# Modulation chains as the moving operand of their sums, and pooling moved from GpSimd to VectorE

## The chip, the cores and the metric

One core of one Trainium2 chip. The metric is the device time of one execution, in microseconds (us); the median of three runs stands for the kernel. The profile is of one further execution.

## The reference, cut to what matters

Two transformer stacks run one after the other on 256 tokens (X) of width 1024, the first with 256 context tokens (CTX) beside them. All is float32. The parts that the change touches are the modulation vectors of four sets (two layers of the first stack, two of the second), and the pooling branch of the first layer:

```python
mod = (silu_c @ ada_w[i] + ada_b[i])[:, None, :]      # ada_w[i]: 1024 x 6144
mod_c = silu_cc @ ada_w[i] + ada_b[i]
sh1, sc1, gt1, sh2, sc2, gt2 = jnp.split(mod, N_MOD, axis=-1)
...
for gi, w in enumerate(POOL_WINDOWS):                 # 2, 4, 8, 16
    lo = jnp.clip(t - w // 2, 0, L)
    hi = jnp.clip(t + w // 2, 0, L)
    ...
    mean = (jnp.take(csg, hi, axis=1) - jnp.take(csg, lo, axis=1)) / (hi - lo)[None, :, None]
    outs.append((mean - uf[..., sl]).astype(u.dtype) @ pool_w[gi])
```

A product of one vector (or of two, where the context needs its own) with a 1024 x 6144 matrix, four times over; and for each of four groups of 128 features a windowed mean less the value itself.

## The kernel before, in words

**Weights and queues.** All large weights come as blocks of 1 MB through a ring of four slots, in one written order (`block_order`, L215). SyncE issues the loads (`load_blocks`, L412): block j waits until block j - 4 is used. Each engine has a program of its own, written out at the end of the kernel; `step` marks an event on a semaphore and `wait_ge(*after(event))` waits for one. A `mod` block is 256 columns of a modulation matrix: 24 of them make a set. The order puts 16 further blocks of set 0 (after the first eight) between the blocks of the first projection (`ev_in`) and of the first output projection (`ev_out`), sets 1 and 2 into the first feed-forward network (`mlp1_0`, `mlp2_0`, in four quarters of an up and a down half, both segments, 512 tokens), and set 3 into the second (`mlp1_1` up, `mlp2_1` down, 256 tokens).

**Chains and sums.** Four of the first eight mod blocks are multiplied on TensorE (`mod_block`, L580). All others are a chain on VectorE (`mod_chain`, L594): the eight 128-row slices of the block, each times one column of silu(c), added up elementwise (L613, L616). With two vectors (set 0 and a third of set 1) the chain keeps one accumulator of 128 x 256 per vector. With one vector it keeps two accumulators, for even and odd slices, and adds them at the end (L620). TensorE then sums over the 128 partitions (`mod_sum`, L626): the accumulator is the stationary operand, 128 columns at a time, and one column of ones moves (L635). The result is one column of PSUM bank 7 per 128 outputs. Chains reuse their buffers: a chain waits for the sum of the chain two before it (the first eight) or four before it. `side_blocks` (L460) places the sums in TensorE's program ahead of the matmuls of the next block. `mod_vectors` (L660) adds the biases chunk by chunk on VectorE (L679), applies the gains (L687), and frees bank 7 for the next set.

**Split matmuls.** The large products run as three matmuls of rounded operands. ScalarE rounds a block (`high`, L506), VectorE makes the remainder (`low`, L515), and TensorE multiplies (`columns`, L537). VectorE's chains stand in block order ahead of the remainder of the block that follows them (`side_chains`).

**Pooling.** GpSimd (`pool_pool`, L1211) waits for the four pooled tiles of the first projection (`taken ev_in 3`), then runs for each of the four groups one to four doubling adds (L1225), a product with the inverse counts (L1230) and a subtraction (L1232). `pool_tensor` (after both attentions) multiplies the results.

**Attention.** `att_tensor`, `att_vector` and `att_scalar` run 16 units (head, half of the queries) each for the latent and then the context attention. In unit i VectorE takes the scores out of PSUM and finds the maxima (L1063 to L1076), then normalises unit i - 1 (L1083, L1097); ScalarE does the exponentials and copies; TensorE does the scores (L1013), transposes (L1023) and values (L1034). In the context attention TensorE also makes filling matmuls (L998).

**Norms.** A norm sums squares on TensorE (L786), takes the root on ScalarE (L802) and the reciprocal on VectorE (L809), and then adds the residual (L898, L903). `mod_vectors` for set 0, chunks 2 to 5, stands in VectorE's program between the first remainders of the network and that reciprocal.

## Time and profile before

| | |
|---|---|
| median of 3 runs | 2556.5 us (2555.28 to 2557.27) |
| the profiled execution | 2558.39 us |
| its span | 2556.6 us |
| TensorE busy (PE) | 2362.8 us, 92% of the span |
| VectorE busy (DVE) | 1715.2 us, 67% |
| ScalarE busy (ACT) | 1020.0 us, 40% |
| GpSimd busy (POOL) | 67.1 us, 3% |

The profile names engines PE, PEld (weight loads of TensorE), DVE, ACT, POOL and SP. A line such as L616 is the line of the kernel that issued the instruction; lines inside a helper serve all its callers. The chain of waits is followed back from the last instruction: each piece is what the end waited for at that time. A float32 matmul appears as two records, each with a weight load. Durations of matmuls in the timeline include their way through the array, so neighbours overlap; the chain of waits shows them from end to end. PEclk is the granted clock of TensorE as a share of 2.4 GHz.

### The profile page before, as it was taken

Reading aid. Unit: us, or ns where it says so; the run is one execution under the profiler, and the core shown is the slowest. Engines: PE = TensorE matmul, PEld = TensorE weight load, DVE = VectorE, ACT = ScalarE, POOL = GpSimd, SP = SyncE. Lnnn points to the kernel's source line nnn. Section 1 sums busy time; section 2 is a strip of 40 time slices with the busy share of each in tenths; the row PEclk is TensorE's granted clock in tenths of the full one; section 3 lists DMA queues with packets and bytes.
Section 4 is the critical chain, followed back from the end, with each engine's and each line's share of the span. In section 5 each row is a group of like instructions: output and inputs, shape, how many; then the busy total and the mean of one; then the engine's idle time right before and its main releaser. Section 6 shows DMA issues by size and latency. Waiting matters only on the chain.

```text
span 2556.6 us, 46809 instructions
## 1 busy us (share of the span) xinstructions
PE 2362.8 (92%) x20170; PEld 1952.1 (76%) x20170; DVE 1715.2 (67%) x3302; ACT 1020.0 (40%) x1893; POOL 67.1 (3%) x70
## 2 busy tenths in 40 slices
PE   6899989999998999999999889898989989998997
PEld 5675467888875578889887789894777888677886
DVE  5966779677646247887763777756356865745576
ACT  2225243323322224544432453334245653644465
POOL 0300000000000000000000000020000011000000
PEclk9899989999998999999999999899899999997999
DMA  7330426665542100000003577550056943003574
GB/s 310 133 131 1 158 106 222 230 256 216 213 155 75 57 1 3 3 4 3 11 4 118 200 273 294 188 182 1 9 206 230 345 165 132 1 1 132 181 303 191
DMA packets 47279, 348.02 MB, mean 136 GB/s; under 512 B 5248, under 2 KB 5248, under 8 KB 5728
## 3 DMA queue, kind: packets, MB, share of 16 engines
q1 hardware_dynamic: 45936, 334.52, 35.1%
q0 software_dynamic: 1136, 10.51, 1.0%
q8 instruction: 158, 2.59, 0.4%
q14 instruction: 49, 0.40, 0.0%
HBM read 343.96 MB, written 1.05 MB: 135 GB/s over the span
## 4 chain that ended last, share of the span: by engine, by line
PE 76%; DVE 16%; ACT 6%; issue 2%; DMA 1%; DVEq 0%; ACTq 0%; POOLq 0%
PE banks L537 23%; PE banks L932 9%; PE banks L1852 6%; DVE arena L616 3%; PE banks L2708 3%; PE banks L2709 3%; PE banks L2710 3%; PE banks L786 2%; PE banks L1718 2%; PE banks L1034 2%; PE banks L1013 2%; PE banks L1929 1%; PE banks L2739 1%; PE banks L2741 1%; PE banks L2740 1%
## 5 line engine op out<-in xcount | busy, mean ns | idle before, releaser
L616 DVE SCALAR_TENSOR_TENSOR arena<-weight_slots,silu_c,arena 128x256 f32<-128x256 f32 x776 | 328.1, 492 | 0.0
L515 DVE TENSOR_TENSOR moe_w_low<-weight_slots,moe_w_high 128x2048 fp32r<-128x2048 f32 x96 | 217.9, 2289 | 70.4 <-ACT moe_w_high L506 69.5
L932 PE MATMUL banks<-arena,weight_slots 128*128 128x256 f32 (+1 forms) x768 | 229.6, 457 | 13.5 <-DVE arena L1599 11.7
L932 PEld LDWEIGHTS banks<-arena,weight_slots 128*128 128x128 f32 x768 | 148.3, 194 | 88.7 <-issue 73.6
L506 ACT ACTIVATE mlp_w_high<-weight_slots 128x2048 fp32r<-128x2048 f32 x64 | 122.3, 1911 | 178.3 <-PE banks L537 105.4
L506 ACT ACTIVATE moe_w_high<-weight_slots 128x2048 fp32r<-128x2048 f32 x96 | 181.2, 1911 | 23.8 <-PE banks L2741 19.7
L515 DVE TENSOR_TENSOR mlp_w_low<-weight_slots,mlp_w_high 128x2048 fp32r<-128x2048 f32 x64 | 146.3, 2286 | 49.2 <-ACT mlp_w_high L506 49.1
L1852 PE MATMUL banks<-weight_slots,arena 64*64 64x64 f32 (+1 forms) x3648 | 147.0, 223 | 18.9 <-ACT arena L1872 13.3
L1852 PEld LDWEIGHTS banks<-weight_slots,arena 64*64 64x64 f32 x3648 | 138.9, 135 | 27.2 <-ACT arena L1872 15.2
L2708 PE MATMUL banks<-moe_w_high,slots_x 128*128 128x512 f32 x320 | 133.2, 416 | 11.8 <-DVE moe_w_low L515 11.8
L2709 PE MATMUL banks<-moe_w_low,slots_x 128*128 128x512 f32 x320 | 129.2, 404 | 0.0
L2710 PE MATMUL banks<-moe_w_high,slots_x 128*128 128x512 f32 x320 | 128.8, 403 | 0.0
L1117 ACT ACTIVATE arena<-arena 128x256 f32<-128x256 f32 (+2 forms) x160 | 71.9, 450 | 104.6 <-DVE arena L1076 104.6
L786 PE MATMUL banks<-arena,constants 128*128 128x256 f32 (+1 forms) x224 | 75.8, 476 | 20.3 <-ACT arena L830 20.3
L2080 ACT ACTIVATE weight_slots<-banks 128x512 f32<-128x512 f32 x80 | 46.9, 595 | 118.5 <-DVE weight_slots L2259 92.6
L1929 PE MATMUL banks<-weight_slots 64*64 64x64 f32 x2560 | 83.6, 220 | 9.2 <-DVE weight_slots L2296 9.2
L1034 PEld LDWEIGHTS banks<-arena 128*64 128x64 f32 (+2 forms) x520 | 55.6, 139 | 42.0 <-issue 23.6
L1929 PEld LDWEIGHTS banks<-weight_slots 64*64 64x64 f32 x2560 | 78.9, 135 | 11.2 <-DVE weight_slots L2296 11.2
L613 DVE TENSOR_SCALAR arena<-weight_slots,silu_c 128x256 f32<-128x256 f32 x184 | 58.0, 356 | 37.4 <-PE banks L635 18.3
L1034 PE MATMUL banks<-arena 128*64 128x128 f32 (+2 forms) x520 | 80.3, 285 | 2.6 <-ACT arena L1135 1.4
L2708 PEld LDWEIGHTS banks<-moe_w_high,slots_x 128*128 128x128 f32 x320 | 61.8, 193 | 25.8 <-ACT moe_w_high L506 9.7
L2296 DVE TENSOR_TENSOR weight_slots<-banks,constants 128x512 f32<-128x512 f32 x80 | 54.2, 688 | 40.4 <-PE banks L1852 40.4
(392 smaller groups left out, 5196.6 us busy)
## 6 DMA issues: line engine op xcount, KB each, us to landing
weight_slots<-weights SPq DMA_DIRECT2D x318, 1024.0 KB, 4.8
arena<-small POOLq DMA_DIRECT2D x1, 2560.0 KB, 9.0
arena<-x_t POOLq DMA_DIRECT2D x1, 2048.0 KB, 15.9
arena<-bias POOLq DMA_DIRECT2D x1, 2048.0 KB, 9.5
constants<-consts POOLq DMA_DIRECT2D x1, 1410.0 KB, 21.2
out_t<-arena SPq DMA_DIRECT2D x1, 1024.0 KB, 3.9
parameters<-params POOLq DMA_DIRECT2D x1, 775.0 KB, 9.2
arena<-pool_inv POOLq DMA_DIRECT2D x1, 512.0 KB, 10.4
```

The source lines that it names most:

```text
L506: nc.scalar.activation(self.pair(j)[0], slot(j, 0, SLOT), ACT.Copy).then_inc(*act.step("high", j))
L515: nc.vector.tensor_tensor(self.pair(j)[1], slot(j, 0, SLOT), self.pair(j)[0], ALU.subtract).then_inc(*v.step("used", j))
L537: ins = nc.tensor.matmul(out, self.pair(j)[part][:, at:at + P], x(k), start=start and n == 0 and k == 0, stop=stop and n == 2 and k == til ...
L616: nc.vector.scalar_tensor_tensor(a_, w, c, a_, ALU.mult, ALU.add).then_inc(*v.step())
L786: ins = nc.tensor.matmul(psum(SUMS_BANK[segs[-1]], 0, len(segs) * SEQ), cn("ones"), squares_of(key, segs, k), start=(k == 0), stop=(k == K ...
L932: ins = nc.tensor.matmul(psum(b, 0, w), slot(j, k, 256, i * P, P), moving(k), start=(k == 0), stop=(k == KT - 1))
L1034: ins = nc.tensor.matmul(psum(b, 0, P, rows), v, T[0:w, u % 2, i * P:(i + 1) * P], start=(i == 0), stop=(i == len(vs) - 1))
L1852: ins = nc.tensor.matmul(psum(b, n * width, width, r), lhs, rhs, start=(i == 0), stop=(i == len(ts) - 1))
L1929: ins = nc.tensor.matmul(psum(b, p * 64, 64, r), Z[r, p, :], XI[r, p, :], start=False, stop=True, skip_group_check=True)
L2708: nc.tensor.matmul(psum(b), x_hi, wh, start=(k == 0), stop=False)
L2709: nc.tensor.matmul(psum(b), x_hi, wl, start=False, stop=False)
L2710: ins = nc.tensor.matmul(psum(b), x_lo, wh, start=False, stop=(k == KT - 1))
```

## The change

- A chain's sum has the accumulators as moving operand (256 columns) and a 24-column matrix as stationary operand, which has ones in column n and zeros elsewhere. Chain n thus lands in row n of a 24-row block of PSUM bank 7, 256 columns per vector. With one vector TensorE adds both accumulators into the same row, and VectorE's add (L620) is gone. This holds for all chains but those of the first eight blocks.
- When the 24 rows of a set are there, VectorE copies them to SBUF (`mod_rows_vector`), in the place of the last chain's accumulators, and TensorE transposes them back into columns (`mod_turn`). `mod_vectors` then adds all biases of a vector in one instruction. The buffer of a set's last chain is free only after the turn.
- The block order in the first network puts all of set 1 ahead of the last block of the second down quarter, and the first block of set 2 behind the first up block after it.
- The pooling instructions run on VectorE, one after each of units 2 to 13 of the latent attention and 2 to 7 of the context attention. GpSimd keeps only the clearing of the padded tiles.
- A constant of 47 columns is added.

```diff
--- before.py
+++ after.py
@@ -44,7 +44,8 @@
 for _n, _w in (("ident", 128), ("ones", 128), ("block_ones", 128), ("swap", 128), ("cos", 256), ("sin", 256),
                ("causal", 128), ("cmp_mask", 2 * N_CMP), ("cmp_live", 2), 
                ("order", 2 * 128), ("first_level", 2 * 64), ("later_levels", 2 * 5 * 64), ("ident64", 64),
-               ("scan_keep", 512), ("tie", 4), ("eps", 2), ("heads", 30)):
+               ("scan_keep", 512), ("tie", 4), ("eps", 2), ("heads", 30),
+               ("one_row", 47)):
     _const(_n, _w)
 N_CONST = sum(w for _, w in CONST_COLS.values())
@@ -88,6 +89,7 @@
     c["tie"] = np.broadcast_to(np.array([4.0, 3.0, 2.0, 1.0]), (P, 4))
     c["eps"] = np.broadcast_to(np.array([RMS_EPS, GN_EPS]), (P, 2))
     c["heads"] = (np.arange(30)[None, :] == 14 + i[:, None] // HD)
+    c["one_row"] = np.broadcast_to(np.arange(47) == 23, (P, 47))
     out = np.concatenate([np.asarray(c[n], np.float64).reshape(P, w) for n, (_, w) in CONST_COLS.items()], 1)
     return np.ascontiguousarray(out.astype(np.float32))
@@ -216,8 +218,9 @@
     order = ["mod0"] * FIRST_MODS + ["ev_in"] * 2 + mixed(("ev_in", 6), ("mod0", 8)) + mixed(("ev_out", 4), ("mod0", 8))
     order += ["mlp1_0"] * 2 + mixed(("mlp1_0", 2), ("mod1", 3)) + mixed(("mlp2_0", 4), ("mod1", 7))
-    order += mixed(("mlp1_0", 4), ("mod1", 7)) + mixed(("mlp2_0", 4), ("mod1", 7))
-    order += (mixed(("mlp1_0", 4), ("mod2", 6)) + mixed(("mlp2_0", 4), ("mod2", 6))) * 2
+    order += mixed(("mlp1_0", 4), ("mod1", 8)) + mixed(("mlp2_0", 3), ("mod1", 6)) + ["mlp2_0"]
+    order += ["mlp1_0"] + mixed(("mlp1_0", 3), ("mod2", 6)) + mixed(("mlp2_0", 4), ("mod2", 6))
+    order += mixed(("mlp1_0", 4), ("mod2", 6)) + mixed(("mlp2_0", 4), ("mod2", 6))
     order += ["wr"] * 4 + ["wk"] * 4 + ["wv"] * 4 + ["wo"] * 4
     order += mixed(("mlp1_1", 16), ("mod3", 12)) + mixed(("mlp2_1", 16), ("mod3", 12))
     order += ["ev2_in"] * 12 + ["ev2_out"] * 4 + ["moe0"] * 48
@@ -568,12 +571,11 @@
             return (CTX, X) if m == 0 or (m == 1 and n < FIRST_MODS) else (X,)
-        def mod_bank(pe, m):
-            key = ("mod", m, 0)
+        def mod_bank(pe, m, part):
+            key = ("mod", m, part)
             if bank_state["holder"][7] != key:
                 if bank_state["holder"][7] is not None:
-                    held = bank_state["holder"][7]
-                    pe.wait_ge(*after("taken", "mod", held[1], 2 if held[1] == 0 else 0))
+                    pe.wait_ge(*after("taken", *bank_state["holder"][7]))
                 bank_state["holder"][7] = key
                 events.where[key] = 7
@@ -581,7 +583,7 @@
             m, n = mod_of(j)
             pe.wait_ge(*after("silu_c"))
-            mod_bank(pe, m)
+            mod_bank(pe, m, 0)
             pe.wait_ge(*after("block", j))
             for i in range(2):
                 t = 2 * n + i
@@ -599,7 +601,9 @@
             v.wait_ge(*after("block", j))
             slots = 2 if v.chains < 8 else 4
             if j >= FIRST_MODS and v.chains >= slots:
-                v.wait_ge(*after("mod_summed", *v.chained[v.chains - slots]))
+
+                m_, n_ = v.chained[v.chains - slots]
+                v.wait_ge(*(after("mod_turned", m_) if n_ == 23 else after("mod_summed", m_, n_)))
             vecs = mod_vecs(m, n)
             for k in range(KT):
                 w = slot(j, k, 256)
@@ -615,17 +619,55 @@
                         v.wait_ge(v.own[0], v.own[1] - 1)
                         nc.vector.scalar_tensor_tensor(a_, w, c, a_, ALU.mult, ALU.add).then_inc(*v.step())
             v.mark("used", j)
-            if len(vecs) == 1:
-                v.wait_ge(*v.own)
-                nc.vector.tensor_tensor(acc[:, 0], acc[:, 0], acc[:, 1], ALU.add).then_inc(*v.step())
             v.mark("mod_acc", m, n)
             if j >= FIRST_MODS:
                 v.chained.append((m, n))
                 v.chains += 1
+        def in_rows(m, n):
+
+            return m > 0 or n >= FIRST_MODS
+
+        def first_row(m):
+            return FIRST_MODS if m == 0 else 0
+
+        def mod_row(pe, m, n):
+
+
+            mod_bank(pe, m, part_of(m))
+            pe.wait_ge(*after("mod_acc", m, n))
+            acc = chain_sums[m, n]
+            pe.wait_ge(*after("consts"))
+            vecs = mod_vecs(m, n)
+
+            for a_, s in enumerate(vecs if len(vecs) == 2 else vecs * 2):
+                ins = nc.tensor.matmul(psum(7, s * 256, 256, ROWS_24), cn("one_row", 23 - n, 24), acc[:, a_],
+                                       start=(n == first_row(m) and a_ == 0), stop=True, skip_group_check=True)
+            ins.then_inc(*pe.step("mod_summed", m, n))
+
+        def mod_rows_vector(v, m):
+
+
+            v.stage("mod")
+            v.wait_ge(*after("mod_summed", m, 23))
+            at_ = 256 * mod_vecs(m, first_row(m))[0]
+            nc.vector.tensor_copy(rows_of(m)[:, at_:512], psum(7, at_, 512 - at_, ROWS_24)).then_inc(*v.step("mod_rows", m))
+
+        def mod_turn(pe, m):
+
+            pe.wait_ge(*after("mod_rows", m))
+            for s in mod_vecs(m, first_row(m)):
+                for i in range(2):
+                    ins = nc.tensor.transpose(psum(7, (2 * s + i) * 24, 24), rows_of(m)[:, s * 256 + i * P:s * 256 + i * P + P],
+                                              cn("ident", 0, 24, ROWS_24))
+            ins.then_inc(*pe.step("mod_turned", m))
+
         def mod_sum(pe, m, n):
-            mod_bank(pe, m)
+            if in_rows(m, n):
+                mod_row(pe, m, n)
+                return
+            mod_bank(pe, m, 0)
             pe.wait_ge(*after("mod_acc", m, n))
             acc = chain_sums[m, n]
             pe.wait_ge(*after("consts"))
@@ -644,6 +686,12 @@
         chain_sums.update({mod_of(j): OUT_ACC[:, i % 4] for i, j in enumerate(rest[8:16])})
         chain_sums.update({mod_of(j): MACC[:, i % 4] for i, j in enumerate(rest[16:])})
+        ROWS_24 = slice(0, 24)
+        part_of = lambda m: 2 if m == 0 else 0
+
+        def rows_of(m):
+            return chain_sums[m, 23][ROWS_24].rearrange("p a b -> p (a b)")
+
         def side_chains(v, j_next):
             while v.at_block < j_next:
@@ -660,7 +708,8 @@
         def mod_vectors(v, m, chunks=range(6)):
             v.stage("mod")
-            v.wait_ge(*after("mod_summed", m, 4 * chunks[-1] + 3))
+            rows = in_rows(m, 4 * chunks[0])
+            v.wait_ge(*(after("mod_turned", m) if rows else after("mod_summed", m, 4 * chunks[-1] + 3)))
             v.wait_ge(*after("params"))
             M = MOD[m]
             src = psum(7, 0, 2 * MOD_TILES).rearrange("p (t s) -> p t s", s=2)
@@ -672,7 +721,14 @@
             else:
                 gains[1] = (pr("norm1_g2", (m - 2) * KT, KT), 1.0)
                 gains[4] = (pr("norm2_g2", (m - 2) * KT, KT), 1.0)
-            for chunk in chunks:
+            for s in (mod_vecs(m, 4 * chunks[0]) if rows else ()):
+
+                n0, n1 = 4 * chunks[0], max(n for n in range(24) if s in mod_vecs(m, n)) + 1
+                part = M[:, 2 * n0:2 * n1, s].rearrange("p (n i) -> p i n", i=2)
+                b = bias_at[:, 2 * n0:2 * n1].rearrange("p (n i) -> p i n", i=2)
+                got = psum(7, 48 * s, 48).rearrange("p (i n) -> p i n", i=2)[:, :, n0:n1]
+                nc.vector.tensor_tensor(part, got, b, ALU.add).then_inc(*v.step())
+            for chunk in (() if rows else chunks):
                 vecs = mod_vecs(m, 4 * chunk)
                 t, s = slice(chunk * KT, (chunk + 1) * KT), slice(vecs[0], vecs[-1] + 1)
                 b = bias_at[:, t].unsqueeze(2).to_broadcast([P, KT, len(vecs)])
...
@@ -1208,28 +1264,34 @@
             g.wait_ge(*after("read", KT - 1))
             g.eng.dma_start(SORT, small[:, 6656:6656 + N_SORT]).then_inc(*g.step("sorting", by=16, sem="sorting_loaded"))
-        def pool_pool(g):
+        def pool_pads(g):
             g.stage("pooling")
             nc.gpsimd.memset(UP, 0.0).then_inc(*g.step("pads"))
-            g.wait_ge(*after("taken", "ev_in", 3))
-            g.wait_ge(*after("pool_inv"))
-            for gi in range(4):
-                u = UP[:, gi]
-                src, shifts = u, []
-                for lv in range(gi + 1):
-                    dst = PT3[:, lv % 2]
-                    up, down = (0, 1) if lv == 0 else (1 << (lv - 1), 1 << (lv - 1))
-                    lo, hi = 1 << lv, 288 - (1 << lv)
-                    g.wait_ge(*g.own)
-                    nc.gpsimd.tensor_tensor(dst[:, :, lo:hi], src[:, :, lo + up:hi + up],
-                                            src[:, :, lo - down:hi - down], ALU.add).then_inc(*g.step())
-                    src = dst
-                g.wait_ge(*g.own)
+
+        def pool_steps():
+
+
+            return [(gi, lv) for gi in range(4) for lv in range(gi + 3)]
+
+        def pool_vector(v, gi, lv):
+
+            u = UP[:, gi]
+            src = u if lv == 0 else PT3[:, (lv - 1) % 2]
+            if (gi, lv) == (0, 0):
+                v.wait_ge(*after("taken", "ev_in", 3))
+                v.wait_ge(*after("pool_inv"))
+            v.wait_ge(*v.own)
+            if lv <= gi:
+                up, down = (0, 1) if lv == 0 else (1 << (lv - 1), 1 << (lv - 1))
+                lo, hi = 1 << lv, 288 - (1 << lv)
+                nc.vector.tensor_tensor(PT3[:, lv % 2][:, :, lo:hi], src[:, :, lo + up:hi + up],
+                                        src[:, :, lo - down:hi - down], ALU.add).then_inc(*v.step())
+            elif lv == gi + 1:
                 inv = PINV[:, gi].unsqueeze(1).to_broadcast([P, 2, SEQ])
-                nc.gpsimd.tensor_tensor(PD[:, gi], src[:, :, 16:272], inv, ALU.mult).then_inc(*g.step())
-                g.wait_ge(*g.own)
-                nc.gpsimd.tensor_tensor(PD[:, gi], PD[:, gi], u[:, :, 16:272], ALU.subtract).then_inc(*g.step("pooled", gi))
+                nc.vector.tensor_tensor(PD[:, gi], src[:, :, 16:272], inv, ALU.mult).then_inc(*v.step())
+            else:
+                nc.vector.tensor_tensor(PD[:, gi], PD[:, gi], u[:, :, 16:272], ALU.subtract).then_inc(*v.step("pooled", gi))
         def pool_tensor(pe):
             pe.stage("pooling")
@@ -1419,6 +1481,8 @@
                         ins.then_inc(*pe.step("x02_part", q, g))
                         if i == 1:
                             pe.mark("multiplied", j)
+                        if q % 2 and g == KT - 2:
+                            mod_turn(pe, 1 + q // 2)
                         if q == 3 and g >= 3:
                             sums_tensor(pe, "y_x02", BOTH, g - 3)
                 if q == 1:
@@ -1465,6 +1529,9 @@
             v.stage("mlp0")
             for n in range(32):
                 q, r = divmod(n, 8)
+                if n % 16 == 15:
+                    mod_rows_vector(v, 1 + n // 16)
+                    v.stage("mlp0" if n == 15 else "mlp0b")
                 MLP0.low(v, n + MLP0.ahead)
                 if r < 4:
                     for f in (8 * q + 2 * r, 8 * q + 2 * r + 1):
@@ -1509,9 +1576,10 @@
                 pe.mark("x12_down", g)
                 if g >= 2:
                     sums_tensor(pe, "y_x12", ONE, g - 2)
+            side_blocks(pe, block_of["ev2_in"][0], 0)
+            mod_turn(pe, 3)
             for g in range(KT - 2, KT):
                 sums_tensor(pe, "y_x12", ONE, g)
-            side_blocks(pe, block_of["ev2_in"][0], 0)
         def mlp_split_scalar(act):
@@ -1558,6 +1626,8 @@
             for i in range(16):
                 MLP.low(v, 16 + i + MLP.ahead)
             side_chains(v, block_of["ev2_in"][0])
+            mod_rows_vector(v, 3)
+            v.stage("mlp_down")
             EV2.low(v, 0)
...
@@ -3257,7 +3327,7 @@
         def _(eng):
             g = queue(eng, "gpsimd")
             loads_pool(g)
-            pool_pool(g)
+            pool_pads(g)
             load_low_rank(g)
             ev2_pool(g)
             od_pool(g)
@@ -3284,6 +3354,7 @@
             project_tensor(pe, "x01", "ev_out", lambda k: CAT[:, :, k, :], cat_ready, BOTH,
                            banks=range(6),
                            then=y_sums(pe, "x01", BOTH, lambda: side_blocks(pe, block_of["mlp1_0"][0], 0)))
+            mod_turn(pe, 0)
             x_sums_tensor(pe, "n2_0", [X, CTX])
             mlp0_tensor(pe)
             x_sums_tensor(pe, "n1_1", ONE)
@@ -3400,11 +3471,16 @@
             EV_IN.low(v, 0)
             low_vector(v, "n1_0", 0, 0, BOTH, BOTH[::-1])
             ev_in_vector(v)
-            att_vector(v, LAT)
-            att_vector(v, CON)
+            pooling = pool_steps()
+            def pool_next(n):
+                for _ in range(n):
+                    pool_vector(v, *pooling.pop(0))
+            att_vector(v, LAT, {i: lambda: pool_next(1) for i in range(2, 14)})
+            att_vector(v, CON, {i: lambda: pool_next(1) for i in range(2, 8)})
             v.stage("norm")
             MLP0.low(v, 0)
             MLP0.low(v, 1)
+            mod_rows_vector(v, 0)
             mod_vectors(v, 0, range(2, 6))
             v.stage("norm")
             for seg in (X, CTX):
```

## Rows read from the trace of the kernel before

**Rows 1.** Busy time by stretch, all engines; from, length, then busy us (instructions).

```profile
core 0: us, PE busy (x) PEld busy (x) DVE busy (x) ACT busy (x) POOL busy (x), PEclk, DMA share, GB/s
100.00:125.00 25.00, 16.65 (x82) 13.90 (x80) 25.00 (x30) 5.51 (x5) 16.29 (x13) 0.89 0.14 45
...
460.00:560.00 100.00, 99.58 (x465) 82.64 (x464) 74.99 (x150) 29.18 (x34) 0.00 (x0) 1.00 0.63 236
```

**Rows 2.** Timeline, first projection: start, us, engine, line, what, count, [idle before].

```profile
84.89 5.63 DVE L616 SCALAR_TENSOR_TENSOR arena<-weight_slots,silu_c,arena 128x256 f32<-128x256 f32 x14
...
95.87 2.60 DVE L613 TENSOR_SCALAR arena<-weight_slots,silu_c 128x256 f32<-128x256 f32 x2
...
98.39 19.13 DVE L616 SCALAR_TENSOR_TENSOR arena<-weight_slots,silu_c,arena 128x256 f32<-128x256 f32 x14
...
117.57 1.05 PE L635 MATMUL banks<-constants,arena 128*128 128x1 f32 x8 [3.34 <-DVE arena L616]
...
123.63 1.87 PE L635 MATMUL banks<-constants,arena 128*128 128x1 f32 x8 [5.01 <-DVE arena L616]
```

**Rows 3.** Chain of waits, first projection: start, us, what, records.

```profile
125.84 13.01 PE banks L537 x48
138.85 0.79 PE banks L635 x8
139.63 11.05 PE banks L537 x48
...
163.10 1.68 PE banks L635 x16
```

**Rows 4.** Chain of waits, first norm after attention.

```profile
332.18 2.61 PE banks L635 x24
334.79 3.49 PE banks L786 x4
...
338.81 1.76 DVE arena L809
...
340.67 1.29 DVE arena L898 x2
...
342.75 0.60 DVE arena L898
```

**Rows 5.** Timeline, VectorE in two latent units and one context unit.

```profile
202.24 0.42 DVE L1063 TENSOR_SCALAR arena<-banks 128x256 f32<-128x256 f32 x1 [0.40 <-PE banks L1013]
...
204.90 0.42 DVE L1063 TENSOR_SCALAR arena<-banks 128x256 f32<-128x256 f32 x1 [0.40 <-PE banks L1013]
...
238.33 0.42 DVE L1063 TENSOR_SCALAR arena<-banks 128x256 f32<-128x256 f32 x1 [0.91 <-PE banks L1013]
```

**Rows 6.** Busy time by stretch, first norm after attention; columns as in rows 1.

```profile
334.70:335.50 0.80, 0.80 (x2) 0.43 (x3) 0.64 (x7) 0.00 (x0) 0.00 (x0) 0.50 1.05 440
```

**Rows 7.** Groups by line: count, busy us, mean ns, idle before.

```profile
L635 PE MATMUL banks<-constants,arena 128*128 128x1 f32 x480 | 60.4, 245 | 9.6 <-DVE arena L616 8.3 <-DVE modulations L679 1.2
...
L620 DVE TENSOR_TENSOR arena<-arena 128x256 f32<-128x256 f32 x64 | 27.2, 425 | 2.2
```

**Rows 8.** Chain of waits, both networks and the output projection between them.

```profile
562.57 0.47 DVE modulations L679 x6
...
563.08 0.61 PE banks L635 x4
...
574.72 0.79 PE banks L635 x8
...
586.55 0.34 PE banks L635 x4
...
1388.11 3.45 PE banks L932 x16
...
1459.09 0.42 DVE arena L620
...
1581.71 5.86 PE banks L537 x48
```

**Rows 9.** Busy time by stretch of L635 alone, second network's down half.

```profile
1550.00:1640.00 90.00, 5.53 (x44) 6.08 (x44) 1.00 0.80 298
```

More of the change, by code:

```diff
@@ L989, in fill_ready @@
             if held is not None and held[0] == "mod":
-                pe.wait_ge(*after("taken", "mod", held[1], 2 if held[1] == 0 else 0))
+                pe.wait_ge(*after("taken", *held))
             elif held is not None:
@@ L2651, in moe_tensor @@
             held = bank_state["holder"][7]
-            pe.wait_ge(*after("taken", *((*held[:2], 2 if held[1] == 0 else 0) if held[0] == "mod" else held)))
+            pe.wait_ge(*after("taken", *held))
             def unread(n):
```

## The prediction

> **What bounds the kernel now.** I first read the busy time by stretch, to see which engine fills which stage. In most of the first feed-forward network TensorE is busy for 99.6 of 100 us at full clock, with VectorE at 75: what is added to TensorE there lands on the end of the kernel, what is taken from VectorE does not [rows 1]. The stretch from 100 to 125 us is the opposite: TensorE is busy for 16.65 of 25 us, VectorE for all 25, and GpSimd, nearly idle elsewhere, for 16.29 [rows 1]. The timeline shows why. Fourteen multiply-adds of a modulation chain take 5.63 us as a rule, but 19.13 us from 98.39 on, and the two products ahead of them 2.60 us where they otherwise need some 0.6: exactly while GpSimd pools [rows 2]. TensorE then sits idle for 3.34 us and again for 5.01 us before it has the sums [rows 2], and when it resumes, 48 matmuls take 13.01 us where the next block's take 11.05, because the granted clock had fallen to the lower level [rows 3].
>
> **Pooling off GpSimd, in the projection.** Without the pooling, a chain of two vectors costs 6.1 us (5.6 + 0.5). VectorE's order is chain 3 (begun at 95.87 today), chain 4, rounding remainder of block 4. Chain 3 ends near 102. Chain 4 has two buffers and waits for the sum of chain 2, which TensorE makes after block 2, near 103 (114.2 less one block of 11.05); so it ends near 109.2 and the remainder near 111.5. TensorE ends block 3 at 114.2 (117.57 less the 3.34 idle) [rows 2], so it no longer waits: it sums two chains (1.7 us) and starts block 4 at 116.0 instead of 125.84. That is 9.9 us, and 2.0 us more for the warm clock: **-11.8 us** [rows 3]. I went on through the block order for chains 5 to 8: each ends before TensorE needs it, so the gain should stay. Bounds: -8 (chains a little late again) and -12.5.
>
> **Pooling onto VectorE, in attention.** Ten adds, four products and four subtractions move. VectorE needs 0.60 us of pitch for a two-input instruction of 512 elements, and 0.69 until its result stands: two take 1.29 [rows 4]. Up to 572 elements make that 0.66, and each waits for its own engine's last result, those 0.09 more: 0.75 us. Twelve of them come one per unit in the latent attention, six in the context attention. A latent unit takes 2.66 us (from 202.24 to 204.90), of which VectorE idles 0.40 until the scores are there [rows 5]; that idle figure counts to the end of the last instruction, so a unit becomes 2.26 + 0.09 + 0.60 to 0.66, about 2.94: 0.28 more. The first two units are slower anyway, and about 0.2 us of lead is used up first: 10 x 0.28 - 0.2 = **+2.6 us**. In the context attention the idle time is 0.91 us a unit [rows 5], more than 0.75: nothing. It costs 0 if the pitch hides better, and 18 x 0.75 = +13.5 if nothing does.
> The Trainium skill (VectorE: DVE Perf Modes, section on the TRN2 errata) gives a float32 tensor_tensor of N elements (N + 151)/0.96 ns, an estimated 0.75 us for 572. The rows give a close figure as duration, 0.69 for 512; I use the shorter pitch where nothing waits.
>
> **The sums of chains.** Before the change a chain half is the stationary operand, loaded 128 columns at a time against one column of ones. The profile has two records per float32 matmul. 480 records are 240 matmuls: four for each two-vector chain, two for a one-vector chain (64 of these, by the 64 halves added on VectorE), [rows 7]. On the chain of waits a pair of one-vector chains costs 0.79 us and a single one 0.34 [rows 8]; a two-vector chain costs 0.79 and a pair 1.68 [rows 3]. After the change each chain of either kind is two matmuls with 256 moving columns, four records. The nearest row is the plain float32 matmul with 256 moving columns: 16 records in 3.45 us, 0.216 each [rows 8]. So each chain costs 0.86 us, a pair 1.73. The 24-column load should hide.
> - Two-vector chains (24): 0.79 to 0.86, or 1.68 to 1.73; about **+0.6 us**.
> - One-vector chains in the first network (40). On the chain of waits stand 15 pairs and 7 singles, 14.2 us; three more hide where TensorE waits for ScalarE at the start of a down half. By the new order I count 16 pairs and 4 singles on the path: 16 x 1.73 + 4 x 0.86 = 31.1. **+16.9 us.** TensorE has no slack there [rows 1], so this is the largest term. Ends: +3.4 (rival A) and +19.
> - The new order lets an up block follow the second down quarter before any chain of the next set. TensorE now waits there for VectorE's add and six modulation adds until 563.08, 1.2 us [rows 8]: **-1.2 us**.
> - Second network, down half: 11 sums (44 records) [rows 9], each 0.34 to 0.86, on a TensorE that is busy throughout: **+5.7 us**.
> - Second network, up half: the other 13. There VectorE is in the path: chain, add of the halves, remainder, then TensorE. The removed add is 0.42 us plus its wait [rows 8], and the chain of waits crosses about ten; TensorE's longer sums fall into its waits for that remainder. **-3.5 us**, between -4.4 and +2 should TensorE take over.
> - Turning the rows back: 8 records for each of the first two modulation sets, 4 for the other two, at 0.1 each (as the small ones above). Sets 1 to 3 lie on the path: 0.8 + 0.35 + 0.35 = **+1.5 us**. VectorE's copies of the rows come beside a tile's worth of matmuls, so I cost them at nothing; if that cover went, about 0.6 us each.
>
> **The first norm after attention.** TensorE makes 24 tiny records in 2.61 us, then 4 wide ones in 3.49 us, twice the usual time [rows 4]: the granted clock is 0.50, the 1.2 GHz level, right after the tiny ones [rows 6]. With 256 columns moving the sums cost the same 2.6 us, and I expect the full clock, 1.7 us less. Against it, set 0 must now be turned (0.85 us) after the last sum, and VectorE has to make the modulation vectors (some 0.6 us) before its reciprocal at 338.81 [rows 4], where they were made earlier, under the sums. Together 338.2: **-0.6 us**. If the clock still falls: +2.0. If turning hides: -1.8.
> The Trainium skill (TensorE: Matmul & The Clock Gate, Part 4) says that PE-mode transposes do not count as busy for the clock; that would leave the norm where the second end has it, and no row here tells it.
>
> Nothing changes on the weight queue but the order of blocks; GpSimd's later loads come after the first network anyway.
>
> **Sum:** -11.8 + 2.6 + 0.6 + 16.9 - 1.2 + 5.7 - 3.5 + 1.5 - 0.6 = +10.2 us. The profiled execution took 2558.4, so 2568.6; the median of the runs is 2556.5, 1.9 lower, so **2566.7 us**.
>
> **Rivals.**
> A. *The wide sums are cheap (faster).* If a record with a narrow stationary operand runs like the one-pass matmuls with 256 columns, 48 in 5.86 us or 0.122 each [rows 8], a chain costs 0.49 us. The first network then adds 16 x 0.98 + 4 x 0.49 - 14.2 = 3.4, the down half 1.7, and the two-vector chains give back some 7: 13.5 + 4.1 + 7.6 less than above, about -15 us, **2541.5**. It decides from about 0.18 us a record downward, where the sum reaches zero. For it: nothing shows 24 stationary columns. Against: every float32 row with 256 or 512 columns goes by the moving columns alone. Chance 0.12.
> The Trainium skill (TensorE: Matmul & The Clock Gate, Back-to-back issue gap) gives 262 cycles, 109 ns, for 256 columns without telling float32 apart; by it a pair costs an estimated 0.87 us and the sum comes out faster still, near 2537. The float32 row shows twice that.
> B. *VectorE becomes the bound of attention.* If its units get all 0.75 us, with ScalarE and TensorE strung behind it: +13.5 in place of +2.6, **2577.6**. For: 0.40 us idle only. Against: the context units idle 0.91. Chance 0.11.
> C. *Covers and clock pay more.* If the attention hides its steps (-2.6), the norm gives 1.2 more, and the extra sums of a quarter of the places fall into waits (-4): +2.4, **2559**, within 0.2%. Chance 0.15.
> D. *The pooling was not what slowed VectorE.* Then the -11.8 is missing: +22, **2578.5**. Against: slow and fast chains change over with GpSimd's work. Chance 0.04.
>
> **Numbers.** The forecast has 0.58. Its own terms spread over about 2562 to 2573. A measurement of this kernel can tell some 0.2%, 5.1 us, from no change: slower is above 2561.6, faster below 2551.4. Slower: 0.58 + 0.11 + 0.04 = 0.73; same 0.15; faster 0.12. The range from 2557 to 2577.5 takes in case C and the near side of B, and leaves out A and D and a little more.
>
> **What would show it.** Right: no stretch of slow multiply-adds near 100 us, block 4 starting near 116; latent units of about 2.9 us; sums as x4 or x8 groups of 0.86 or 1.73 us on the chain, the first network some 16 us longer; the second network's up half shorter and its down half longer. Wrong: sums of 0.5 us a chain, units still at 2.66 or beyond 3.4, a new wait of TensorE for the row copies, or an up half bound by TensorE.

## The result, and the profile after

| | before | after |
|---|---|---|
| median of the runs | 2556.28 us (2555.28 to 2557.27, 4 runs) | 2581.41 us (2577.56 to 2583.37, 4 runs) |
| the profiled execution | 2558.39 us | 2583.36 us |
| its span | 2556.6 us | 2581.3 us |

The ratio is 1.0096, 95% interval 1.0084 to 1.0108: the change costs 25 us, where +10 had been forecast. First the page of the changed kernel, busy time by engine.

```profile
PE 2407.2 (93%) x20086; PEld 1931.8 (75%) x20086; DVE 1686.9 (65%) x3244; ACT 1022.7 (40%) x1893; POOL 42.1 (2%) x52
```

VectorE has 28 us less to do and GpSimd 25 us less; TensorE has 44 us more, and TensorE is what counts. Its chain of waits in the first projection (start, us, what, records), to be held against [rows 2, 3]:

```profile
89.30 0.97 PE banks L644 x4
90.27 11.15 PE banks L540 x48
...
113.53 1.84 PE banks L644 x8
115.37 11.10 PE banks L540 x48
```

L540 are the split matmuls, L644 the new sums. The gaps and the slow stretch of 13.01 us are gone, and block 4 starts at 115.37 (125.84 before, 116.0 forecast). The timeline of VectorE in the same place has every chain at its usual pace:

```profile
94.50 5.63 DVE L620 SCALAR_TENSOR_TENSOR arena<-weight_slots,silu_c,arena 128x256 f32<-128x256 f32 x14
102.50 0.61 DVE L617 TENSOR_SCALAR arena<-weight_slots,silu_c 128x256 f32<-128x256 f32 x2 [2.36 <-PE banks L644]
```

It is now VectorE that waits for TensorE (2.36 us), not the other way round. The same chain of waits in the first norm after attention [rows 4], in the first network and in the up half of the second [rows 8]:

```profile
326.55 2.70 PE banks L644 x12
329.25 1.91 PE banks L842 x4
332.25 1.67 DVE arena L865
...
436.30 1.84 PE banks L644 x8
438.14 11.10 PE banks L540 x48
...
558.21 0.35 PE banks L661 x4
558.57 16.54 PE banks L540 x72
575.10 1.84 PE banks L644 x8
...
1453.39 0.97 PE banks L644 x4
1454.36 5.94 PE banks L540 x48
...
1468.59 0.76 DVE hidden_low L1624 x2
1469.36 0.53 DVE arena L617 x2
1469.88 2.38 DVE arena L620 x6
1472.26 2.22 DVE mlp_w_low L518
...
1474.52 6.02 PE banks L540 x48
```

L661 are the transposes that turn the rows, L842 the norm's own sums, L865 its reciprocal. A pair of sums takes 1.84 us where 1.73 was forecast, a single one 0.97 where 0.86 was. The reciprocals serve as marks in both kernels, so the time can be told stage by stage. "First attention" is the latent and the context attention of the first layer together, up to the first matmul of the pooling. The first network runs from the last of the three reciprocals of its norm (353.7 us before, 347.05 after) to the reciprocal of the next norm (758.5 and 772.7). The second network (from 1418.9 and 1433.2) and the stages of the second stack are also counted between reciprocals. The two columns on the right are the changed kernel's two profiled executions (the second is the run `changed_again` below):

| stage | before | after | again |
|---|---|---|---|
| start to first attention's first scores | 176.39 | 164.82 | |
| first attention | 86.5 | 91.7 | 88.6 |
| reciprocal of the first norm stands at | 338.8 | 332.2 | |
| first network | 404.8 | 425.6 | 424.7 |
| second network | 220.9 | 226.5 | 226.4 |
| second stack's first attention | 182.4 | 185.0 | 184.9 |
| first expert network | 235.5 | 237.0 | 237.0 |

### The profile page after: what moved, and what is told of

Read it like the earlier page. It is cut to its first block, busy times and chain, and to the rows that moved or that the text cites. A ratio compares the mean times of both kernels' runs of the same rounds, so it can differ in the third digit from the quotient of the medians.

```text
span 2581.3 us, 46560 instructions
## 1 busy us (share of the span) xinstructions
PE 2407.2 (93%) x20086; PEld 1931.8 (75%) x20086; DVE 1686.9 (65%) x3244; ACT 1022.7 (40%) x1893; POOL 42.1 (2%) x52
## 4 chain that ended last, share of the span: by engine, by line
PE 79%; DVE 13%; ACT 6%; issue 1%; DMA 1%; DVEq 0%; ACTq 0%; POOLq 0%
PE banks L540 26%; PE banks L988 9%; PE banks L1922 6%; PE banks L644 3%; PE banks L2778 3%; PE banks L2779 3%; PE banks L2780 3%; PE banks L842 2%; PE banks L1788 2%; PE banks L1090 2%; PE banks L1069 2%; PE banks L1999 1%; PE banks L2809 1%; PE banks L2811 1%; PE banks L2810 1%; DVE arena L620 1%
## 5 line engine op out<-in xcount | busy, mean ns | idle before, releaser
L620 DVE SCALAR_TENSOR_TENSOR arena<-weight_slots,silu_c,arena 128x256 f32<-128x256 f32 x776 | 315.3, 483 | 0.0
L988 PE MATMUL banks<-arena,weight_slots 128*128 128x256 f32 (+1 forms) x768 | 229.4, 457 | 13.5 <-DVE arena L1669 11.8
L1922 PE MATMUL banks<-weight_slots,arena 64*64 64x64 f32 (+1 forms) x3648 | 147.0, 223 | 19.1 <-ACT arena L1942 13.5
L842 PE MATMUL banks<-arena,constants 128*128 128x256 f32 (+1 forms) x224 | 75.0, 472 | 20.3 <-ACT arena L886 20.3
L617 DVE TENSOR_SCALAR arena<-weight_slots,silu_c 128x256 f32<-128x256 f32 x184 | 56.5, 351 | 49.5 <-PE banks L644 30.5
L1999 PEld LDWEIGHTS banks<-weight_slots 64*64 64x64 f32 x2560 | 78.9, 135 | 11.2 <-DVE weight_slots L2366 11.2
L644 PE MATMUL banks<-arena,constants 128*24 128x256 f32 x352 | 87.2, 382 | 0.0
## 6 DMA issues: line engine op xcount, KB each, us to landing
arena<-x_t POOLq DMA_DIRECT2D x1, 2048.0 KB, 16.6
```

The lines of the kernel that those rows point to most:

```text
L620: nc.vector.scalar_tensor_tensor(a_, w, c, a_, ALU.mult, ALU.add).then_inc(*v.step())
L644: ins = nc.tensor.matmul(psum(7, s * 256, 256, ROWS_24), cn("one_row", 23 - n, 24), acc[:, a_], start=(n == first_row(m) and a_ == 0), sto ...
L988: ins = nc.tensor.matmul(psum(b, 0, w), slot(j, k, 256, i * P, P), moving(k), start=(k == 0), stop=(k == KT - 1))
L1922: ins = nc.tensor.matmul(psum(b, n * width, width, r), lhs, rhs, start=(i == 0), stop=(i == len(ts) - 1))
L1999: ins = nc.tensor.matmul(psum(b, p * 64, 64, r), Z[r, p, :], XI[r, p, :], start=False, stop=True, skip_group_check=True)
```

## The experiments

All times are medians in us; each ratio is to the kernel before, run on the same chip beside it.

**The pooling alone.** `pool_only` is the kernel before with the pooling part of the diff and nothing else. `sums_only` is the changed kernel with the pooling back on GpSimd. `pool_gap` takes the 18 instructions to another place, all at once ahead of the first unit:

```diff
-            att_vector(v, LAT, {i: lambda: pool_next(1) for i in range(2, 14)})
-            att_vector(v, CON, {i: lambda: pool_next(1) for i in range(2, 8)})
+            for step_ in pool_steps():
+                pool_vector(v, *step_)
+            att_vector(v, LAT)
+            att_vector(v, CON)
```

> The kernel before with the pooling part alone of the change (sums and block order as before). Theory 1 (the two parts add up, each at the price read in the changed kernel's trace): the attention's end shifts by -6.4 us there (-11.6 in the projection, +5.2 in the latent attention), so 2550, ratio 0.9975. Rival (the latent attention's extra 2.6 us over the 2.6 forecast is a matter of when the clock rises and differs from run to run): 2545 to 2551, and the latent units are 2.95 us either way. Rival (moving the pooling is itself what made the changed kernel slow, by clock dips later on): over 2560.

> The changed kernel with the pooling back on GpSimd: sums, turns and block order of the change alone. Theory 1: +20.7 us in the first network, +6.1 in the second, and up to +4 of later differences: 2583 to 2588, ratio 1.0105 to 1.0125. Rival (the later +4 us come from the sums through the clock and belong to this part): 2588. Rival (sums and pooling hurt only together): below 2575.

> The kernel before with all 18 pooling steps on VectorE in one go between the last remainder of the first projection and the first attention unit, where VectorE sat idle for 17.6 us before L1063. Theory 1: 18 x 0.75 = 13.5 us fit in the gap, the latent units are back at 2.66 us, so only the projection's gain is left: 2556.3 - 11.6 = 2544.7, ratio 0.9955. Rival (the shift of the start by itself costs what the clock gives, the pooling steps having nothing to do with it): latent attention some 2.6 us longer than before all the same, 2547.

Measured: `pool_only` 2546.82, ratio 0.9965 (0.9952 to 0.9977), 9.3 us faster than before; `pool_gap` 2544.74, 0.9955 (0.9938 to 0.9971); `sums_only` 2590.50, 1.0136 (1.0119 to 1.0153), 9.1 us slower than the changed kernel and 2.5 above what was expected of it. The timeline of VectorE in `sums_only` has the slow chain back:

```profile
94.48 2.60 DVE L617 TENSOR_SCALAR arena<-weight_slots,silu_c 128x256 f32<-128x256 f32 x2
97.00 19.15 DVE L620 SCALAR_TENSOR_TENSOR arena<-weight_slots,silu_c,arena 128x256 f32<-128x256 f32 x14
```

So the pooling part is worth some 9 us with either kind of sums, and the sums cost 34. With all 18 steps ahead of the attention, that takes 86.6 us, as before; with one in each unit it takes 91.6 (`pool_only`), of which some 3 us come from the clock, told below. The whole is 2.1 us faster in `pool_gap`, though the two intervals overlap. The timeline of VectorE shows where the steps go, first in `pool_only`, then in `pool_gap`:

```profile
165.15 0.42 DVE L1063 TENSOR_SCALAR arena<-banks 128x256 f32<-128x256 f32 x1 [17.61 <-PE banks L1013]
```

```profile
160.32 0.69 DVE L1238 TENSOR_TENSOR arena<-arena 128x512 f32<-128x512 f32 x1
164.91 0.42 DVE L1063 TENSOR_SCALAR arena<-banks 128x256 f32<-128x256 f32 x1 [3.90 <-PE banks L1013]
```

VectorE idles 17.61 us until the first scores are there. All the pooling fits into that with 3.90 us to spare.

**How much is the second matmul of a chain?** `one_half` lets VectorE add the halves again and TensorE sum one:

```diff
+            if len(vecs) == 1:
+                v.wait_ge(*v.own)
+                nc.vector.tensor_tensor(acc[:, 0], acc[:, 0], acc[:, 1], ALU.add).then_inc(*v.step())
...
-            for a_, s in enumerate(vecs if len(vecs) == 2 else vecs * 2):
+            for a_, s in enumerate(vecs):
```

> The changed kernel, but VectorE adds the two halves of a one-vector chain as before and TensorE sums one of them: 2 records in place of 4. Theory 1 (a sum costs 0.216 us a record plus about 0.11 once per group): a single costs 0.54 in place of 0.97, a pair 0.97 in place of 1.84; 36 chains on the path of the first network give back 15.6 us, the second network 5 to 9: 2557 to 2561. Rival (the cost is per chain, in the change of operands, and not per record): a single stays above 0.75, and the whole above 2568.

Measured: 2561.30, 1.0020 (1.0011 to 1.0030). The first network takes 409.0 us, 16.6 less than in the changed kernel. Its chain of waits there has a pair in four records in place of eight:

```profile
457.79 0.97 PE banks L647 x4
458.77 11.14 PE banks L540 x48
```

16.6 us is 38 times 0.43 us (two records of 0.216), and that network has 40 one-vector chains: the price per record with 256 columns moving, which the main term was built on, holds.

**Is the 24-column load free?** The four kernels below change only the number of stationary columns, and the place of the 47-column constant in its table. The added columns are other constants, and the rows of PSUM that they fill are never read. `wide_stationary`:

```diff
-                ins = nc.tensor.matmul(psum(7, s * 256, 256, ROWS_24), cn("one_row", 23 - n, 24), acc[:, a_],
+                ins = nc.tensor.matmul(psum(7, s * 256, 256), cn("one_row", 23 - n, 128), acc[:, a_],
```

`narrow_last` has 128 columns for sets 0 to 2 and 24 for set 3, `wide_last` the reverse, `stationary_64` has 64 for all.

> The changed kernel with 128 stationary columns in a sum in place of 24 (the columns beyond the 24 hold other constants, their rows of PSUM are never read). Theory 1 (a group of sums costs 0.97 and 1.84 us and not 0.86 and 1.73 because of the narrow load: it cannot be taken under the matmul before, and the next wide load not under it): groups fall to 0.86 and 1.73, the matmuls behind them to 11.05 and 5.86, some 60 groups on the path: 7 to 10 us faster than the changed kernel, 2572 to 2575. Rival (the extra is the change of operand type between rounded and plain float32, which only showed less with one moving column): groups stay at 0.97 and 1.84, 2581.

> 128 stationary columns in the sums of sets 0 to 2, 24 in those of set 3 (second network). Theory 3 (24 stationary columns cost about 0.11 us in the group and 0.2 in the matmuls behind it, wherever they are; the last 4 us come from the narrow sums too): the first network as in the wide run (418.0 us from mark to mark), the second network 226.5 in place of 220.7. The second stack's stages are 2.6 and 1.5 us longer if the last narrow sums before them decide: 2569 to 2570; if earlier ones do, as in the wide run: 2565.5.

> The mirror image: 24 columns in sets 0 to 2, 128 in set 3. Theory 3: the first network 425.6 us, the second 220.7; the second stack's stages as before if the last narrow sums decide (2569), 4 us longer if earlier ones do (2573).

> 64 stationary columns in all sums. Theory 3a (any stationary operand narrower than the full 128 columns keeps loads from being taken under the neighbouring matmuls): as with 24 columns, groups of 0.97 and 1.84, 2579 to 2581. Theory 3b (the price goes by the number of columns): halfway, near 2570. Rival (only the smallest loads are affected): 2560.

| | stationary columns, sets 0 to 2 / set 3 | median | ratio | first network | second network |
|---|---|---|---|---|---|
| changed kernel | 24 / 24 | 2581.41 | 1.0096 (1.0084 to 1.0108) | 425.6 | 226.5 |
| stationary_64 | 64 / 64 | 2575.06 | 1.0080 (1.0063 to 1.0097) | 425.4 | 227.0 |
| narrow_last | 128 / 24 | 2569.42 | 1.0052 (1.0035 to 1.0069) | 416.9 | 225.7 |
| wide_last | 24 / 128 | 2567.82 | 1.0051 (1.0034 to 1.0067) | 424.6 | 220.6 |
| wide_stationary | 128 / 128 | 2559.71 | 1.0011 (1.0002 to 1.0021) | 418.0 | 220.7 |

More than five times as many columns make the kernel 21.7 us faster, where 7 to 10 had been expected. Between the two profiles 13.4 us lie in the two networks (7.6 and 5.8), 1.8 and 1.2 in the projections ahead of and behind the first attention; 2.9 in that attention and 4.0 in two stages of the second stack, whose code does not differ, go with the clock, told below. Each network goes by the width in its own stage and not by the other's; the same code differs by 1.1 us between two kernels (418.0 and 416.9). With 64 columns the networks are no faster than with 24. That `stationary_64` is 6.3 us below the changed kernel as a whole is seen in the same stages that go with the clock: its profile has 88.5 us for the first attention, and the two later stages as before the change. The chain of waits of `wide_stationary` in the first network:

```profile
442.18 1.73 PE banks L643 x8
443.90 10.90 PE banks L539 x48
```

and that of `stationary_64`:

```profile
445.46 1.87 PE banks L643 x8
447.33 11.10 PE banks L539 x48
```

With 128 columns a pair costs exactly the forecast 1.73 us, and the 48 matmuls behind it 10.90; with 24 it is 1.84 and 11.10, with 64 1.87 and 11.10. That is 0.31 us for each group, and the 25 groups on the first network's path make 7.8 of the measured 7.6 us (425.6 less 418.0). The timeline of the changed kernel's weight loads (PEld), and then of its matmuls, at one pair:

```profile
462.11 1.42 PEld L644 LDWEIGHTS banks<-arena,constants 128*24 128x24 f32 x8 [0.35 <-issue]
463.95 1.68 PEld L540 LDWEIGHTS banks<-both_high,mlp_w_high 128*128 128x128 f32 x8 [0.42 <-DVE arena L617]
...
462.11 1.91 PE L644 MATMUL banks<-arena,constants 128*24 128x256 f32 x8
463.95 2.11 PE L540 MATMUL banks<-both_high,mlp_w_high 128*128 128x512 f32 x8
```

and the same views of `wide_stationary`:

```profile
454.41 1.72 PEld L643 LDWEIGHTS banks<-arena,constants 128*128 128x128 f32 x8
456.15 1.79 PEld L539 LDWEIGHTS banks<-both_high,mlp_w_high 128*128 128x128 f32 x8
...
454.64 1.89 PE L643 MATMUL banks<-arena,constants 128*128 128x256 f32 x8
456.18 2.19 PE L539 MATMUL banks<-both_high,mlp_w_high 128*128 128x512 f32 x8
```

With 128 columns the loads run on without a break: the first load of the sums stands 0.23 us ahead of its matmul. With 24 the loads stand idle for 0.35 and 0.42 us at the two changes of width, and load and matmul are recorded as starting together. The idle time stands where the stationary width changes (the second is put down to VectorE's L617, though no such wait stands there with 128 columns). That a load of another width is not taken under the running matmul is my reading of these rows; the cost by width is measured.

**What else could it be?** `const_only` is the kernel before with the unused 47-column constant, which moves the addresses behind it. `changed_again` is the changed kernel once more, for a second profile.

> The kernel before with the 47 unused constant columns alone, which move every buffer behind them by 188 bytes. Theory 2 (the last 4 us of the change, 2.6 in the second stack's first attention and 1.5 in the first expert network, where the granted clock falls after identical instructions, come with the moved addresses): the same two stages are longer by 2.6 and 1.5 us, 2560. Rival (they come with the sums or with how the clock's window happens to lie, not with the constant): stages as before, 2556.

> The changed kernel once more, for a second profile. Theory 2 and the sums' theory alike: the second stack's first attention is again 2.6 us and the first expert network 1.5 us longer than before. Rival (chance in the clock): at least one of them is as before. The latent attention begins at half clock again for some 22 us, or, if that is chance, for 11 us, which would make it 2.6 us shorter.

Measured: `const_only` 2556.88, 0.9998 (0.9988 to 1.0007), with stages as before: addresses are out. `changed_again` 2579.26, 1.0086 (1.0066 to 1.0106). Its first attention took 88.6 us where the first profile had 91.7. One stretch of 10 us of it in the changed kernel's first profile (columns as in [rows 1]):

```profile
175.00:185.00 10.00, 10.00 (x30) 5.67 (x30) 6.30 (x16) 3.56 (x11) 0.00 (x0) 0.51 0.01 2
```

and of its second:

```profile
175.00:185.00 10.00, 9.92 (x50) 5.92 (x49) 8.52 (x23) 4.48 (x12) 0.00 (x0) 0.93 0.01 2
```

The same program stays at the lower clock (0.51) for most of this stretch in one execution and leaves it early (0.93) in the other: 3 us, by execution.

**The new order, and a version that beats both.** `gap_order` is `pool_gap` with the new block order and the old sums. `gap_order_up` goes on from it: for the 13 chains of the second network's up half, where VectorE is in the path, VectorE's add goes, and TensorE adds the second half in the old form, with one moving column:

```diff
-            if len(vecs) == 1:
+            if len(vecs) == 1 and not (m == 3 and n < 13):
...
+            both = m == 3 and n < 13
             for i in range(2):
                 for a_, s in enumerate(mod_vecs(m, n)):
                     at_ = 2 * (2 * n + i) + s
                     ins = nc.tensor.matmul(psum(7, at_, 1), acc[:, a_, i * P:(i + 1) * P],
-                                           cn("ones", 0, 1), start=True, stop=True)
+                                           cn("ones", 0, 1), start=True, stop=not both)
+                    if both:
+                        ins = nc.tensor.matmul(psum(7, at_, 1), acc[:, 1, i * P:(i + 1) * P],
+                                               cn("ones", 0, 1), start=False, stop=True)
```

> Pooling in one go before attention (as in the run pool_gap), sums as before, and the block order of the change. Theory 1: TensorE no longer waits 1.2 us for the modulation vectors of set 1 after the second down quarter, and the sums cost 0.79 and 0.34 as before: 2544.7 - 1.2 = 2543.5. Rival (the six modulation adds return as a wait at the next sum): 2544.7.

> The run gap_order, with VectorE's add of the halves taken away in the 13 chains of set 3 that lie in the second network's up half; TensorE adds both halves there, but with one moving column as before (8 records in place of 4, 0.79 us in place of 0.34). Tests the term of -3.5 us by itself: if VectorE's add is on the path there, the second network falls from 220.9 us by 3 to 4.4 us and the kernel to 2539.5; rival (TensorE takes over as the bound, as it did in the changed kernel): 220 us or more, 2543.

Measured: `gap_order` 2543.05, 0.9945 (0.9929 to 0.9962); its first network takes 402.7 us against 404.9 in `pool_gap`, so the order is worth 2.2 us there, though between the whole kernels 1.7 us is within the spread. `gap_order_up` 2539.11, 0.9930 (0.9913 to 0.9946), the lowest median of all, 17 us below the kernel before; its interval overlaps that of `gap_order`, but its second network takes 215.7 us against 220.9. Its chain of waits there:

```profile
1451.78 6.02 PE banks L538 x48
1457.81 0.12 PE banks L637 x2
1457.92 0.22 PE banks L640 x2
...
1458.59 5.86 PE banks L538 x48
...
1478.39 6.01 PE banks L538 x48
```

A chain's sum, from 1457.81 to 1458.59, is 0.78 us with one column moving, 0.19 less than the 0.97 of the changed kernel, and the matmuls behind it take 5.86 instead of 5.94.

## Why the prediction was right or wrong

| step | forecast | measured |
|---|---|---|
| pooling off GpSimd, to the first scores | -11.8 | -11.6 and -11.2 |
| pooling in the attention | +2.6 | +2.1 and +5.2 in two executions |
| first network, all its terms | +17.0 | +20.8 and +19.9 |
| second network, up half | -3.5 | -2.7 and -2.8 |
| second network, down half with its turn (5.7 + 0.35) | +6.05 | +8.3 and +8.3 |
| two later stages that the change does not touch | 0 | +4.0 and +4.0 |
| the whole | +10.2 | +25.1 by medians |

**Pooling off GpSimd: right**, down to block 4 at 115.37 (forecast 116.0). Rival D is out: `sums_only` has the slow chain, `pool_only` not.

**Pooling onto VectorE: right in kind.** A latent unit went from 2.66 to 2.95 us (forecast 2.94), as the timeline of VectorE in the changed kernel shows:

```profile
200.76 0.42 DVE L1119 TENSOR_SCALAR arena<-banks 128x256 f32<-128x256 f32 x1
...
203.05 0.74 DVE L1288 TENSOR_TENSOR arena<-arena 128x560 f32<-128x560 f32 x1
203.71 0.42 DVE L1119 TENSOR_SCALAR arena<-banks 128x256 f32<-128x256 f32 x1
```

The idle 0.40 us is gone, as in rival B, but not all 0.75 was added, so B's +13.5 did not come. The further 3 us of one execution is clock.

**The wide sums: the step that failed is "The 24-column load should hide".** The moving columns cost what was forecast (`one_half`, and 1.73 a pair in `wide_stationary`); the load does not hide. A group on the path costs 0.11 us more than forecast and the matmuls behind it take 11.10 instead of 11.05: 25 groups at 0.16 are 4.0 us, and the first network came out 3.8 above its terms. The count was near: 17 pairs and 6 singles stand on the chain, 16 and 4 were forecast, but a single at the start of a down half still costs next to nothing (12.36 us from one block's end to the next sum, 12.34 before). With 128 columns, where the load hides, the stage is only 13.2 us longer than before, 3.8 below its terms: the forecast left out that the old sums slow the matmuls behind them (11.05, against 10.90). Rival A is out, its 0.122 us a record against 0.216 in `one_half` and `wide_stationary`.

**The second network: the same step failed, mostly in the down half.** The chain of waits before, in the up half and at the first sum of the down half:

```profile
1461.77 6.03 PE banks L537 x48
...
1475.53 6.04 PE banks L537 x48
...
1550.38 0.34 PE banks L635 x4
```

and after, at the first sum of the down half:

```profile
1561.96 0.97 PE banks L644 x4
```

Counted from the reciprocal (1418.93 and 1433.24), the up half went from 131.5 to 128.7 us: -2.7 where -3.5 was forecast, within its stated ends. Its path was not the forecast one. Before, the chain of waits went once round VectorE every 13.77 us (two blocks). After, it stays on TensorE for three blocks and crosses VectorE once in four: from 1474.52 to 1501.66, or 13.57 us for two blocks. The down half went from 89.4 to 97.7 us: its 11 sums cost 0.63 us more each, where 0.52 was forecast, and the 48 matmuls behind each 0.08, which was not. With 128 columns the two halves take 126.3 and 94.4 us, and two blocks of the up half 13.31, as this chain of `wide_stationary` shows over four blocks:

```profile
1460.13 6.00 PE banks L539 x48
...
1486.74 6.02 PE banks L539 x48
```

In `gap_order_up` it is also 13.31 (1451.78 to 1478.39), and its up half also takes 126.3. So removing VectorE's add is worth 5.2 us in that half, more than forecast, and the narrow loads took back 2.4 of it.

**The clock: two falls that were not forecast.** The second stack's first attention is 2.6 us longer and the first expert network 1.5, on instructions that the change leaves alone. The windows before, and then after at about the same place of the same sequence (columns as in [rows 1]):

```profile
1794.50:1800.50 6.00, 5.12 (x27) 2.81 (x25) 1.94 (x8) 2.66 (x11) 0.00 (x0) 1.00 0.00 0
```

```profile
1814.90:1820.90 6.00, 6.00 (x21) 3.43 (x22) 1.94 (x8) 1.99 (x8) 0.00 (x0) 0.59 0.00 0
```

From 1786.08 us on (1806.83 after) TensorE's timelines agree to 0.01 us up to the fall, which takes some 2.3 of the 2.6 us; then one clock is at 1.00 and the other at 0.59. The longer attention is seen in six profiles, five of them with 24-column sums in the second network, but also in `gap_order_up`, which has no such sums, and not in `stationary_64`. What decides it stays open. The same holds for the expert network, which is longer in four profiles, all with 24 columns for every set (one of them with half the records).

**Norm, order and turns: small, and near.** The norm kept the full clock (1.91 us for four wide records, 3.49 before [rows 4]). From its last group of chain sums to its first reciprocal it went from 6.63 us (332.18 to 338.81) to 5.70 (326.55 to 332.25), a gain of 0.9 where 0.6 was forecast; the output projection ahead of it, with its sums, came out 0.8 longer. The turn stands behind the norm's four wide records (331.16 against 329.25), so this norm does not tell what transposes do to the clock. The turns took 0.35 and 0.23 us in the first network (forecast 0.8 and 0.35), because a transpose shows as one record, 4 and 2 in place of 8 and 4, and no wait for VectorE's copies of the rows stands on the chain. The wait ahead of the third quarter is gone; the order alone brought 2.2 us in its stage where 1.2 was forecast.

The range ended at 2577.5, 3.9 below the result. The load that did not hide makes about 7 us of the missing 15 in the two networks (3.8 and 3.0 above their terms), the clock in the first attention and in the two later stages, a term put at nothing, some 7. With the load hidden (`wide_stationary`) the kernel takes 2559.7 us, 7 below the forecast of 2566.7 and inside the range.

## What to carry to other kernels

Where TensorE is the bound, count the moving columns of a sum over partitions first: here one chain's sum cost 0.34 us with one column moving, 128-column loads included, and 0.86 with 256 moving, at 0.216 us a record. Where a narrow stationary operand stands between wide ones, try it at the full 128 columns: here padding with columns that nobody reads was worth 13.4 us in the two networks. Move work between engines stage by stage, where the trace shows the other one waiting: moving VectorE's adds to TensorE lost time in the network that TensorE bounds, and alone it won 5.2 us where VectorE was in the path.

## What the runs showed of the hardware that was not expected

- A float32 matmul with 24 or 64 stationary columns between matmuls with 128 costs 0.31 to 0.34 us more for each group than one with 128 (1.84 and 11.10 us with 24, 1.87 and 11.10 with 64, against 1.73 and 10.90), and 64 are no better than 24.
- The old sums, with one column moving, also made the 48 matmuls behind them slower, 11.05 us against 10.90 behind 128-column sums with 256 moving. So a group of wide sums costs 0.79 us more than the old pair, less than the 0.94 by which its own duration grew.
- The length of a stretch at the lower clock at the start of the first attention differs between executions of one kernel: the attention took 91.7 and 88.6 us in the changed kernel, and 94.5 in `gap_order_up` against 86.5 in `gap_order`, where its code is the same; that profiled execution (2547.38 us) was the slowest of `gap_order_up`.
